# Encoder layer with 32 experts in float32: bias products placed behind the transposes of the activations, and the down matrix loaded in 8 KB runs with activations stored in a permuted order

## What is computed

```python
def expert_block(args):
    xb, e = args
    gu = xb @ w_gu[e] + b_gu[e]                     # 1024 -> 2048
    g = jnp.minimum(gu[:, :D_EXPERT], SWIGLU_LIMIT)
    lin = jnp.clip(gu[:, D_EXPERT:], -SWIGLU_LIMIT, SWIGLU_LIMIT)
    act = g * jax.nn.sigmoid(SWIGLU_ALPHA * g) * (lin + 1.0)
    return act @ w_down[e] + b_down[e]              # 1024 -> 1024
```

## Time and profile before

| | |
|---|---|
| median of 3 runs | 1594.78 us |
| the profiled execution | 1592.0 us |
| its span, first to last instruction | 1590.1 us |
| TensorE busy | 1558.4 us (98%) |
| VectorE busy | 1276.7 us (80%) |
| ScalarE busy | 1079.7 us (68%) |
| GpSimd busy | 462.9 us (29%) |
| DMA | 467.50 MB, mean 294 GB/s |

### The profile page before, as it was taken

How to read it: one execution, slowest core, us unless ns; L and a number is a source line. 1 busy time by engine, 2 the same in 40 slices (tenths; PEclk the granted TensorE clock), 3 DMA queues, 4 the chain that set the end, 5 groups by cost and what they waited for, 6 DMA issues and landing times.

```text
span 1590.1 us, 22160 instructions
## 1 busy us (share of the span) xinstructions
PE 1558.4 (98%) x7658; PEld 1127.6 (71%) x7658; DVE 1276.7 (80%) x1013; ACT 1079.7 (68%) x968; POOL 462.9 (29%) x254
## 2 busy tenths in 40 slices
PE   8999999999899999999999999999999999999997
PEld 7866688888766666766766777667666766776664
DVE  3768724327689988999999989999998999999884
ACT  6368723224467777877777778777777877777773
POOL 0000200000022733333444333344443333444420
PEclk9999999999999999999999999999999999999999
DMA  7310022437299999999999999999999999999984
GB/s 271 112 60 21 8 89 77 136 119 285 110 354 345 369 378 359 386 377 376 368 368 370 379 371 380 373 375 368 365 371 374 369 379 374 370 376 363 383 314 138
DMA packets 103173, 467.50 MB, mean 294 GB/s; under 512 B 13640, under 2 KB 14176, under 8 KB 70336
## 3 DMA queue, kind: packets, MB, share of 16 engines
q1 hardware_dynamic: 94928, 449.23, 73.6%
q0 software_dynamic: 7872, 17.68, 5.3%
q10 hardware_dynamic: 336, 0.08, 0.0%
HBM read 456.82 MB, written 19.79 MB: 300 GB/s over the span
## 4 chain that ended last, share of the span: by engine, by line
PE 92%; DVE 5%; issue 1%; DMA 1%; ACT 0%; DVEq 0%; POOL 0%; ACTq 0%; POOLq 0%
PE ps L1736 29%; PE ps L1754 14%; PE ps L1739 14%; PE ps L1759 7%; PE ps L1432 6%; PE ps L1434 6%; PE ps L1433 6%; PE ps L1459 4%; DVE l_w L1184 2%; PE ps L1585 1%; DVE head_max L1113 1%; PE ps L1728 1%; PE ps L1541 1%; DVE probs L1131 1%; PE ps L1662 0%
## 5 line engine op out<-in xcount | busy, mean ns | idle before, releaser
L1184 DVE TENSOR_TENSOR l_w<-a_w,h_w 128x2048 fp32r<-128x2048 f32 x384 | 865.8, 2289 | 35.3 <-ACT h_w L829 32.5
L829 ACT ACTIVATE h_w<-a_w 128x2048 fp32r<-128x2048 f32 x384 | 731.2, 1915 | 231.9 <-PE ps L1739 166.7
L964 POOL TENSOR_TENSOR mark_sb<-ones 1x1 f32<-1x1 f32 x93 | 253.2, 2722 | 657.7 <-ACT y_sb L873 648.4
L1736 PE MATMUL ps<-h_w,xt_hi 128*96 128x512 f32 x1024 | 283.9, 399 | 3.6 <-DVE xt_lo L1318 3.6
L1736 PE MATMUL ps<-h_w,xt_lo 128*96 128x512 f32 x1024 | 279.5, 394 | 0.0
L1739 PE MATMUL ps<-l_w,xt_hi 128*96 128x512 f32 x1024 | 279.1, 394 | 0.0
L1736 PEld LDWEIGHTS ps<-h_w,xt_lo 128*96 128x96 f32 x1024 | 166.2, 162 | 71.9
L1739 PEld LDWEIGHTS ps<-l_w,xt_hi 128*96 128x96 f32 x1024 | 166.1, 162 | 71.7
L1736 PEld LDWEIGHTS ps<-h_w,xt_hi 128*96 128x96 f32 x1024 | 161.1, 162 | 74.6 <-issue 7.8
L1754 PE MATMUL ps<-h_w,at_hi 128*96 128x512 f32 x512 | 162.1, 398 | 0.2 <-issue 0.2
L1754 PE MATMUL ps<-h_w,at_lo 128*96 128x512 f32 x512 | 159.5, 392 | 0.0
(11 more groups left out here) (249 smaller groups left out, 1551.4 us busy)
## 6 DMA issues: line engine op xcount, KB each, us to landing
a_w<-in_w_gate_up SPq DMA_DIRECT2D x256, 1024.0 KB, 8.4
a_w<-in_w_down SPq DMA_DIRECT2D x128, 1024.0 KB, 7.8
w_raw<-in_w_in SPq DMA_DIRECT2D x8, 2048.0 KB, 7.9
w_raw<-in_w_out SPq DMA_DIRECT2D x2, 2048.0 KB, 7.5
w_raw<-in_w_in SPq DMA_DIRECT2D x2, 1024.0 KB, 7.8
x_sb<-in_x SPq DMA_DIRECT2D x8, 256.0 KB, 7.3
w_raw<-in_w_mem_kv SPq DMA_DIRECT2D x1, 2048.0 KB, 11.5
x<-in_x SPq DMA_DIRECT2D x4, 512.0 KB, 5.2
```

The lines of the kernel that those rows point to most:

```text
L829: nc.scalar.activation(h_w[m % H_SLOTS][:], a_w[m % A_SLOTS][:], ACT.Copy).then_inc(wh_done, 1)
L964: nc.gpsimd.tensor_tensor(mark_sb[:], ones[0:1, 0:1], ones[0:1, 0:1], ALU.mult).then_inc(marked, 1)
L1184: nc.vector.tensor_tensor(l_w[m % A_SLOTS][:], a_w[m % A_SLOTS][:], h_w[m % H_SLOTS][:].bitcast(F32), ALU.subtract).then_inc(wl_done, 1)
L1736: nc.tensor.matmul(ps[0:SLOTS, n, :], x_part[:, k, :], w_h[:, n * COLS:(n + 1) * COLS], start=False, stop=False)
```

## The change

The bias products leave the head of `gate_up` and run after `between(1)`, behind the transposes of the activations, with their wait. The first product of the first piece opens the accumulation in their place.

The down matrix is read with another assignment of rows to partitions: partition p gets rows 8p to 8p + 7, of which one piece takes two that are neighbours, 8 KB in one run. So that the products fit, the activations are written in a permuted order: column h * 512 + 8p + k goes to place 128k + 64h + p. PSUM is read in order as before; in SBUF the eight values of one p now lie 512 bytes apart. The transposes read 128 neighbouring places, as before. This applies to L859, L1327, L1333 (which also reads `sg_sb` in that order) and L1352.

```diff
@@ -295,6 +295,13 @@
+        def by_down_row(t):
+
+            return t.rearrange("s (k h p) -> s h p k", k=KD, h=2)
+
+        def of_bank_pair(n):
+            return ps[0:SLOTS, n:n + 2, :].rearrange("s h (p k) -> s h p k", k=KD)
@@ -513,7 +520,7 @@
         wgu = w_gate_up[0].rearrange("e (k p) n -> e p k n", p=P)
-        wdn = w_down[0].rearrange("e (k p) n -> e p k n", p=P)
+        wdn = w_down[0].rearrange("e (p k) n -> e p k n", p=P)
@@ -856,7 +863,7 @@
-                nc.scalar.activation(sg_sb[:].rearrange("p (h n) -> p h n", h=2), ps[0:SLOTS, 0:2, :], ACT.Relu, bias=limits[0:SLOTS, 0:1],
+                nc.scalar.activation(by_down_row(sg_sb[:]), of_bank_pair(0), ACT.Relu, bias=limits[0:SLOTS, 0:1],
@@ -1324,13 +1331,13 @@
             def clamp(j):
-                nc.vector.tensor_scalar(act_sb[:].rearrange("p (h n) -> p h n", h=2), ps[0:SLOTS, 2:4, :], LIMIT, -LIMIT,
+                nc.vector.tensor_scalar(by_down_row(act_sb[:]), of_bank_pair(2), LIMIT, -LIMIT,
                                         ALU.min, ALU.max).then_inc(l_ready, 1)
             def activate(j):
                 dve.wait_ge(sg_ready, j + 1)
-                sg = sg_sb[:].rearrange("p (h n) -> p h n", h=2)
-                nc.vector.scalar_tensor_tensor(out=sg, in0=ps[0:SLOTS, 0:2, :], scalar=LIMIT, in1=sg,
+                sg = by_down_row(sg_sb[:])
+                nc.vector.scalar_tensor_tensor(out=sg, in0=of_bank_pair(0), scalar=LIMIT, in1=sg,
                                                op0=ALU.min, op1=ALU.mult).then_inc(gs_ready, 1)
@@ -1349,7 +1356,7 @@
-            nc.vector.tensor_scalar(y_sb[:].rearrange("p (h n) -> p h n", h=2), ps[0:SLOTS, 0:2, :], LIMIT, None, ALU.min).then_inc(gs_ready, 1)
+            nc.vector.tensor_scalar(by_down_row(y_sb[:]), of_bank_pair(0), LIMIT, None, ALU.min).then_inc(gs_ready, 1)
@@ -1722,10 +1729,6 @@
-                pe.wait_ge(bias_row_in[s], 64 * loads)
-                for n in range(4):
-                    rows = slice(32 * n, 32 * n + 2)
-                    nc.tensor.matmul(ps[0:SLOTS, n, :], ones[rows, 0:SLOTS].bitcast(F32R), bias_row[s][rows, :].bitcast(F32R), start=True, stop=False)
                 pe.wait_ge(xt_lo_done, j + 1)
@@ -1733,12 +1736,18 @@
-                            nc.tensor.matmul(ps[0:SLOTS, n, :], x_part[:, k, :], w_h[:, n * COLS:(n + 1) * COLS], start=False, stop=False)
+                            nc.tensor.matmul(ps[0:SLOTS, n, :], x_part[:, k, :], w_h[:, n * COLS:(n + 1) * COLS],
+                                             start=k == 0 and x_part is xt_hi, stop=False)
...
                     between(k)
+                    if k == 1:
+                        pe.wait_ge(bias_row_in[s], 64 * loads)
+                        for n in range(4):
+                            rows = slice(32 * n, 32 * n + 2)
+                            nc.tensor.matmul(ps[0:SLOTS, n, :], ones[rows, 0:SLOTS].bitcast(F32R), bias_row[s][rows, :].bitcast(F32R), start=False, stop=False, skip_group_check=True)
```

## The result

| | before | changed |
|---|---|---|
| median of 18 runs each, same chip | 1594.07 us (1591.86 to 1596.08) | 1597.86 us (1595.47 to 1599.99) |
| ratio, 95% interval | | 1.0024 [1.0017, 1.0030] |
| profiled execution / its span | 1592.0 / 1590.1 us | 1595.63 / 1593.8 us |

The change costs 3.8 us; the forecast was 4.9. In the changed kernel L836 is ScalarE's high part of the weights, L1191 VectorE's low part, L866 the Relu, L1334 the clamp, L1340 the product with the sigmoid, L1359 its stand-in in the first job, L1325 `xt_lo`. TensorE's lines are L1739 and L1743 (gate and up), L1750 (bias), L1763 and L1768 (down) and L1466 (turns).

What follows compares the result with a forecast made beforehand. TensorE was taken to bound the loop, VectorE having 3.1 us of slack a job. Bias in the first jobs 1.2, permuted writes 2.9 and clock 0.8 made +4.9 on 1594.8: 1599.7 us, range 1593.8 to 1603.

Steps and rivals of the forecast that it cites:

- Bias in the loop: Steady expert loop: moved bias products cost 0.60 us a job as before, so the move is worth 0.
- The entry of 0.16: First job, from turns to bias: 0.82 us against 0.66 needed; forecast took 0.10, part being a load after idle time.
- rival D: Bias entry and exit share the turns' pipeline time, writes free: -4.3 us, 1590.5; chance 0.09.
- Bias in the first jobs: First three jobs: bias products lose the cover of TensorE's waits for xt_lo, 1.2 us in sum.
- Permuted writes: Strided writes cost 0.73 us each, like L1265's strided read; four ahead of second and third jobs' xt_lo, 2.9 us.
- lower bound: Price of a strided write could be 0, since a write need not wait for memory as a read does.
- The clock: Third job's start: TensorE may fall to 1.2 GHz after waiting, costing 1.6 or 2.4 us, or nothing; 0.8 taken.
- third wait of 3.2 us: TensorE's empty stretch before the third job grows from 1.7 by 2 x 0.73 to 3.2 us.
- Pieces and tail: 8 KB down pieces are costed at 0, their delay or speed-up hidden; two longer VectorE instructions in the tail are covered, 0.
- The sum: All terms put on the median: 1594.8 + 4.9 = 1599.7 us; 4.1 us before the clock term.
- The waits of the first three jobs: TensorE waits for xt_lo three times, 8 us or so in place of 3.6.
- Rival C: Strided writes much dearer, VectorE becomes the bound from 3.1 us more a job: 39 us, 1634; chance 0.07.

Runs made afterwards that it cites:

- e1: Kernel before with only the bias products moved behind the turns; activations and down pieces unchanged: 1595.29 us, ratio 1.0000 to before.
- e2: Changed kernel with the bias products kept at the head of gate_up; permuted writes and 8 KB pieces stay: 1599.20 us, ratio 1.0025 to before.
- e9: Changed kernel with the token block's xt_lo one low-part product sooner on VectorE (2.2 us): 1595.72 us, ratio 1.0015 to before.
- e5: Changed kernel with the first job's bias products back ahead of its first product: 1596.94 us, ratio 1.0025 to before.
- e4: Kernel before with only the permuted activation writes; down pieces stay 4 KB, so rows and activations don't match: 1599.20 us, ratio 1.0022.
- e3: Kernel before with only the down pieces read as 8 KB runs; activations in old order, so rows don't match: 1594.70 us, ratio 1.0000.
- e8: Changed kernel with one more contiguous clamp a job on VectorE, 1.14 us, result unread: 1608.39 us, ratio 1.0090 to before.
- e11: Changed kernel with both the extra contiguous clamp a job and xt_lo one low product sooner on VectorE: 1598.78 us, ratio 1.0030 to before.
- e10: Kernel before with only xt_lo one low-part product sooner on VectorE: 1593.44 us, ratio 0.9994 to before.

## Why the prediction was right

It was right in sign, in range, and in cause. By its steps:

**Bias in the loop, 0.** Right: 0.58 against 0.60 us, period 35.17. The entry of 0.16 that the first job showed was 0.09 here, so the reading that part of it came from the idle time ahead holds, and rival D's shared entry and exit didn't come. Over 28 periods, from the fourth job's first product to the last job's, the sum is 984.94 us before (540.88 to 1525.82) and 984.76 changed (544.24 to 1529.00). So 0.18 us were won in all, under 0.01 a job, and these are the 0.2 by which the ledger's last part is below the 0.6 of the third job's bias.

**Bias in the first jobs, 1.2.** e1's profile has 0.8, its median is 0.6 above that of before, and its ratio has an interval of 1.4 us to either side. The medians do without the term: the whole change is at 1.0024, and e2, which doesn't move the bias products, at 1.0025. Not contradicted, not shown alone.

**Permuted writes, 4 x 0.73 = 2.9.** The rate from L1265 was right to a tenth: 0.76 on the clamp, 0.67 on L1359 and 0.67 on the clamp next to it in the first job, 0.82 on L1340, which also reads in stride. The read adds at most 0.06 us to the write. In the first to second job, 0.6 of bias and 0.67 + 0.67 make 1.94, measured 1.92. VectorE's stretch from the clamp of the first job to the third job's `xt_lo` went from 40.80 (463.82 to 504.62) to 43.55 us, 2.75 more, where the four durations are 3.0 more. ScalarE's write costs more, 0.98 us; it is off the path in the third job, as e9 shows. The row was a read, and that a write would cost the same was a guess that came true. The reason that the prediction gave for its lower bound, that a write need not wait for memory, had no row behind it, and these writes do not bear it out.

The Trainium skill (VectorE: DVE Perf Modes, section on mode 1x) puts that mode at one result a cycle and says that odd strides work in it. If that is read as free of charge, the runs are against it: these writes went from 1.19 to 1.94 ns an element (1220 and 1985 ns for 1024). The Trainium skill (SBUF — State Buffer, section on the DMA port swizzle, note on cachelines) says that an access which goes to a new line each time pays a penalty; these writes agree with that, if it is meant for writes too.

**The clock, 0.8 of 0 to 2.4.** The forecast took a mean over what is either there or not. It was 0 in the changed kernel's profile (granted clock 1.00 from 505 to 520 us, after 2.07 us of waiting) and in e5's (2.50 us), 1.3 in e2's (2.41) and some 2.4 in e4's (2.54). So the length of the wait alone doesn't settle it. The forecast's third wait of 3.2 us was too long. Of the kernel before:

```profile
474.37 0.82 PE L1459 MATMUL ps<-ident,act_sb 96*128 96x96 f32 x8
...
502.49 1.09 PE L1759 MATMUL ps<-l_w,at_hi 128*96 128x512 f32 x4
```

From the last down products to the third job's first product it is 3.21 us here (502.49 to 505.70) and 3.15 in the changed kernel (505.84 to 508.99). This stretch did not grow, because TensorE's own work ended 3.35 us later. The second job began 1.7 later, its bias products took 0.6 behind the turns, and the low clock at its start lasted longer: up to the turns it is 8.26 us (468.88 to 477.14) in place of 7.21 (467.16 to 474.37). The prediction's sum for this wait had left out these last two, the first of which stands in its own paragraph on the bias products.

**Pieces and tail, 0.** Right. From the last job's first product to the end it is 64.28 us before and 64.80 changed. These 0.52 more are no more than the 0.58 of the bias products that now follow it, so the tail adds nothing. Down pieces land 8.2 us after issue instead of 7.8, and e3 has ratio 1.0000. Packets fell from 103173 to 86789 (the page, part 2), so the runs of 8 KB do exist and have no taker.

**The sum.** In the profiles it is 3.9 us from the turns on, against 4.1 without the clock. The excess of the forecast over the measured 3.8, 1.1 us, is the clock term of 0.8 and 0.3 in the other terms. The waits of the first three jobs sum to 8.7 us, where 8 or so were expected. (The chances named for a slower kernel, 0.43, 0.05 and 0.07, add up to 0.55 and not to 0.53.)

**Rival C was priced at a wrong point.** It was to decide from VectorE's slack a job, 3.1 us more. The chain in the job decides earlier, at the margin of 2.6 us ahead of the wanted `xt_lo`, which stood in the prediction and wasn't used for C. The change took 1.5 of it (`xt_lo` ends at 1070.68, the products start at 1071.79, 1.1 left), e8's 1.14 us exceeded the rest, and e11 gave it back. So 1.14 us more on this chain tipped the loop, in each of some 30 jobs; a third strided write, with 0.8 us more, would still have fitted by these numbers, which no run tried.

## What to carry to other kernels

A layout that makes DMA runs longer is paid for where the data are written or read in stride: ask which engine has slack for it, and whether the transfers had anybody waiting. The slack of an engine per period is not the slack of a chain through it; read from the timeline when the result is done and when it is wanted, also in the first jobs, where queues have not yet run ahead. Work put into a wait must be measured against it record by record: 37 products of ones won nothing, and 16 of them, together with one step moved on VectorE, won 5 us.

## What the runs showed of the hardware

**Strided writes of float32 in SBUF.** With neighbours 512 bytes apart, 1024 elements in each of 96 partitions cost VectorE 0.67 to 0.82 us more on 1.2, and ScalarE 0.98 on 1.11. Reading turns' columns 32 bytes apart costs TensorE 62 ns more a load of 128 columns, on 140.

**GpSimd's records change with what VectorE does, and not only with how much.** GpSimd's busy time, all of it off the path, was 462.9 us before and in e3 462.8, but 629.4 in e4, 637.3 in e2, 644.6 in the changed kernel and 798.7 in e8, whose extra write is contiguous. That looks like growth with VectorE's work, but the order of its queue counts as well. With `xt_lo` one step sooner, GpSimd had 347.2 us in e9 beside the changed kernel's 644.6, at the same work of VectorE (1319.7 and 1317.0 us), and 332.7 in e10 beside 462.9. In e11 it stayed at 797.5. No run tells by which mechanism.

**The releaser of a wait.** The changed kernel's third job waited for VectorE's `xt_lo` (e9), though its row in the profile named ScalarE. The two ended within 0.1 us, 508.86 and 508.87.
